# Expert stage of a streaming encoder step: gathers for pairs of experts, 8 KB weight rows, one weight tile of six in plain fp32, unrolled with two accumulator sets

## What is computed

```python
def moe_ffn(h, ...):                       # h: 320 x 1024
    g_p, g_i = top_k(softmax(h @ w_rg + b_rg), 1)          # one of 4 groups
    e_p, e_i = top_k(softmax(logits of that group's 8 experts), 2)
    gate = g_p * e_p / sum(e_p)
    # for each of 32 experts e, for the tokens t routed to it:
    a, u = split(h[t] @ w_e_in[e], 2)      # w_e_in[e]: 1024 x 1024, two halves of 512
    y = ((silu(a) * u) @ w_e_out[e]) * gate                # w_e_out[e]: 512 x 1024
    # y is added back to the token's row; every token has two choices
x = LN2(alpha * x + (1 + gate2) * moe)
```

## Time and profile before

| | |
|---|---|
| runs (us) | 1332.75, 1337.75, 1338.72 |
| span of the profiled execution (us) | 1332.6 |
| time of that execution by itself | not listed beside the runs; its span is 0.15 us under the fastest run |
| PE busy | 1085.3 us, 81% |
| DVE busy | 963.6 us, 72% |
| ACT busy | 694.6 us, 52% |
| POOL busy | 647.2 us, 49% |
| moved by DMA | 303.33 MB, mean 228 GB/s |

### The profile page before, as it was taken

How to read it: one execution, slowest core, us unless ns; L and a number is a source line. 1 busy time by engine, 2 the same in 40 slices (tenths; PEclk the granted TensorE clock), 3 DMA queues, 4 the chain that set the end, 5 groups by cost and what they waited for, 6 DMA issues and landing times.

```text
span 1332.6 us, 14213 instructions
## 1 busy us (share of the span) xinstructions
PE 1085.3 (81%) x4460; PEld 752.7 (56%) x4460; DVE 963.6 (72%) x1069; ACT 694.6 (52%) x734; POOL 647.2 (49%) x348
## 2 busy tenths in 40 slices
PE   5688899888999999998845788888888788888850
PEld 2355677566786666686634555555555565555540
DVE  3968642456653333456785999999999999999967
ACT  3654231231322222332223688888888788888842
POOL 0423920200010000001804999998999979998740
PEclk8798999998997555697956999999999999999885
DMA  9676333244636100136424799999999999999923
GB/s 333 241 256 233 110 111 135 85 137 146 229 92 214 63 0 0 63 127 205 130 103 124 267 370 363 370 364 367 368 366 366 370 353 366 374 366 368 355 97 118
DMA packets 151813, 303.33 MB, mean 228 GB/s; under 512 B 10740, under 2 KB 10788, under 8 KB 151270
## 3 DMA queue, kind: packets, MB, share of 16 engines
q1 hardware_dynamic: 142040, 282.75, 60.1%
q0 software_dynamic: 9744, 20.19, 5.1%
HBM read 299.97 MB, written 14.73 MB: 236 GB/s over the span
## 4 chain that ended last, share of the span: by engine, by line
PE 33%; POOL 24%; DMA 17%; issue 12%; DVE 10%; ACT 2%; POOLq 1%; SPq 0%; ACTq 0%; DVEq 0%
POOL x_item L732 10%; DMA x_item<-scratch_h,slot_token_now 9%; PE bank L1671 6%; PE bank L1677 6%; PE bank L1673 4%; DMA w_raw<-in_w_in 3%; POOL scratch_y L743 2%; POOL slot_token_now L728 2%; POOL slot_row_now L739 2%; DVE w_lo L1033 2%; PE bank L1704 2%; ACT w_hi L782 1%; DMA scratch_y<-y_item,slot_row_now 1%; DMA w_raw<-in_w_ada 1%; PE bank L1829 1%
## 5 line engine op out<-in xcount | busy, mean ns | idle before, releaser
L1538 DVE TENSOR_TENSOR w_lo<-w_raw,w_hi 128x2048 fp32r<-128x2048 f32 x188 | 432.8, 2315 | 15.6 <-ACT w_hi L939 15.6
L939 ACT ACTIVATE w_hi<-w_raw 128x2048 fp32r<-128x2048 f32 x188 | 354.9, 1904 | 2.1 <-PE bank L1943 1.4
L1033 DVE TENSOR_TENSOR w_lo<-w_raw,w_hi 128x2048 fp32r<-128x2048 f32 x72 | 173.3, 2425 | 136.6 <-ACT w_hi L782 136.4
L782 ACT ACTIVATE w_hi<-w_raw 128x2048 fp32r<-128x2048 f32 x72 | 136.6, 1912 | 209.0 <-PE bank L1677 92.4
L1943 PE MATMUL bank<-w_lo,xT_item 128*128 128x512 f32 x512 | 155.5, 426 | 89.9 <-DVE w_lo L1538 89.9
L732 POOL DMA_INDIRECT x_item<-scratch_h,slot_token_now x32 | 218.5, 6829 | 15.9 <-DMA scratch_y<-y_item,slot_row_now 11.4
L1943 PEld LDWEIGHTS bank<-w_lo,xT_item 128*128 128x128 f32 x512 | 89.0, 192 | 154.8 <-DVE w_lo L1538 142.0
L1940 PE MATMUL bank<-w_hi,xT_item 128*128 128x512 f32 x512 | 149.2, 414 | 6.5 <-ACT w_hi L939 2.6
L1671 PE MATMUL bank<-w_hi,h_hi 128*128 128x512 f32 x384 | 142.1, 411 | 12.7 <-ACT w_hi L782 12.3
L1940 PEld LDWEIGHTS bank<-w_hi,xT_item 128*128 128x128 f32 x512 | 93.4, 192 | 39.4 <-issue 17.0
L728 POOL COPY slot_token_now<-slot_token 64x1 int32 (+1 forms) x32 | 107.7, 3366 | 5.7 <-DMA x_item<-scratch_h,slot_token_now 5.6
(11 more groups left out here) (438 smaller groups left out, 1753.4 us busy)
## 6 DMA issues: line engine op xcount, KB each, us to landing
w_raw<-in_w_e_in SPq DMA_DIRECT2D x128, 1024.0 KB, 5.6
w_raw<-in_w_e_out SPq DMA_DIRECT2D x64, 1024.0 KB, 6.3
w_raw<-in_w_in SPq DMA_DIRECT2D x32, 1024.0 KB, 8.0
w_raw<-in_w_ada SPq DMA_DIRECT2D x24, 1024.0 KB, 6.6
bias_rows<-in_b_in SPq DMA_DIRECT2D x16, 256.0 KB, 4.8
w_raw<-in_w_ret_proj SPq DMA_DIRECT2D x4, 1024.0 KB, 19.2
w_raw<-in_w_fox_proj SPq DMA_DIRECT2D x4, 1024.0 KB, 20.7
w_raw<-in_w_o SPq DMA_DIRECT2D x4, 1024.0 KB, 5.1
```

The lines of the kernel that those rows point to most:

```text
L782: nc.scalar.activation(whi[n % NSPL][:], raw[n % NRAW][:], ACT.Copy).then_inc(hi_done, 1)
L939: nc.scalar.activation(whi[ss][:], raw[rs][:], ACT.Copy).then_inc(hi_done, 1)
L1033: V.tensor_tensor(wlo[n % NSPL][:], raw[n % NRAW][:], whi[n % NSPL][:].bitcast(F32), ALU.subtract).then_inc(lo_done, 1)
L1538: V.tensor_tensor(wlo[ss][:], raw[rs][:], whi[ss][:].bitcast(F32), ALU.subtract).then_inc(lo_done, 1)
```

## The change

The expert stage is written anew:

- Items are experts in a fixed order in which two neighbours form a pair (`expert_of`: 0, 16, 1, 17, ...). One gather brings up to 128 rows, 64 for each of the two, into one of two `xg` buffers, and one scatter takes 128 result rows from one of two `ySb` buffers. POOL's copies of index columns and its `hold` instructions are gone for these.
- The weights' rows are dealt to partitions in blocks ("(p k) n" in place of "(k p) n"), so that a tile is one run of 8 KB a partition in place of four of 2 KB. To match, DVE stores h2 (L1393) and the hidden rows (L1552) permuted.
- A tile j of w_e_in now holds all 1024 columns of two rows a partition, so each of the tiles 0 to 3 feeds both banks, a and u. Tile 2 (`NATIVE`) is not split: PE multiplies it as fp32, with the unsplit 64 rows (`xR`) as the stationary operand.
- The loops are unrolled. a and u have two sets of banks (0, 1 and 2, 3, by the item's parity), the result uses banks 4 and 5, `hidden_T` writes bank 5, and the pair's rows are transposed into banks 6 and 7.
- The splitting of expert 0's tiles in the router's stretch is gone. The rows that come back for the closing stage land in the space of the raw tiles.
- An expert's further items, of which there are none in this data, run in a loop behind.

The diff, cut to its core. First the weights' layout and the order of the loads on SP's queue:

```diff
-    w_in_e = i["w_e_in"][0].rearrange("e (k p) n -> e p k n", p=P)
+    w_in_e = i["w_e_in"][0].rearrange("e (p k) n -> e p k n", p=P)
...
+        for e in range(NE + 1):
+            if e < NE:
+                for j in range(4):
+                    expert_tile(e, j)
+            if e:
+                for j in (4, 5):
+                    expert_tile(e - 1, j)
```

POOL's loop over pairs; a gather of pair q waits for the transposes of pair q-2, a store for the four sums of its pair:

```diff
+        for q in range(2, PAIRS):
+            pool.wait_ge(x_landed, 16 * q)
+            gather(q)
+            if q - 2 < 3:
...
+            if q >= 3:
+                pool.wait_ge(y_written, 16 * (q - 3))
+            store_pair(q - 2)
```

ACT (n counts the split tiles alone, m all tiles):

```diff
+            m, n = tile_at[(e, j)], split_at[(e, j)]
+            act.wait_ge(raw_landed[m % NRAW], 16 * (m // NRAW + 1))
+            act.wait_ge(used, n - NSPL + 1)
...
+        def x_high(q):
+
+            act.wait_ge(x_trans, q + 1)
+            nc.scalar.activation(xR[q % 2][:].rearrange("p k c s -> p (k c s)"), bank[7][:, 0:4 * SLOTS],
+                                 ACT.Copy).then_inc(x_raw, 1)
+            nc.scalar.activation(xT[q % 2][:, 4:6, :, 0:SLOTS], pair_of(bank[7], 4)[:, 2:4], ACT.Copy)
+            nc.scalar.activation(xT[q % 2][:, 0:4, :, 0:SLOTS], pair_of(bank[6], 4), ACT.Copy).then_inc(x_hi, 1)
...
+        for e in range(NE + 1):
+            if e < NE:
+                item_hi(e, 0)
+            if e:
+                lows(e - 1)
+            if e < NE:
+                item_hi(e, 1)
+            if e:
+                silu(e - 1)
+            if e < NE:
+                item_hi(e, 3)
+            if e >= 2:
+                y_low(e - 2)
+            if e:
+                hidden_high(e - 1)
+                item_hi(e - 1, 4)
+                item_hi(e - 1, 5)
+            if e % 2 == 0 and e + 2 < NE:
+                x_high(e // 2 + 1)
```

DVE (the permuted store of h2 first):

```diff
-            st(V.tensor_tensor(ht, ht, m2[0:rows, 0, :], ALU.add), h2_ready)
...
+            st(V.tensor_tensor(ht.rearrange("r (k p) -> r p k", p=P), tmp.rearrange("r (p k) -> r p k", p=P),
+                               m2[0:rows, 0, :].rearrange("r (p k) -> r p k", p=P), ALU.add), h2_ready)
...
+        for e in range(NE + 1):
+            if e < NE:
+                item_lo(e, 0)
+            if e:
+                sums(e - 1)
+            if e < NE:
+                item_lo(e, 1)
+            if e:
+                hidden(e - 1)
+            if e < NE:
+                item_lo(e, 3)
+            if e >= 2:
+                y_sum(e - 2)
+            if e:
+                hidden_low(e - 1)
+                item_lo(e - 1, 4)
+                item_lo(e - 1, 5)
+            if e % 2 == 0 and e + 2 < NE:
+                x_low(e // 2 + 1)
```

PE (`in_product(j)` and `out_product(j)` are eight matmuls of 512 columns, four by `hi` and four by `lo`, and then count up `used`):

```diff
+        def native_product(e, b, X):
+
+            m = tile_at[(e, NATIVE)]
+            pe.wait_ge(raw_landed[m % NRAW], 16 * (m // NRAW + 1))
+            for kk in range(2):
+                for half in range(2):
+                    last = mm(bank[b + half][0:SLOTS, :], X[kk], wide(raw[m % NRAW])[:, kk, 512 * half:512 * half + 512],
+                              start=False, stop=False)
+            last.then_inc(nat_used, 1)
...
+            if e < NE:
+                pe.wait_ge(x_split, q + 1)
+                if e >= 2:
+                    pe.wait_ge(u_drained, e - 1)
+                in_product(0)
+                in_product(1)
+            if e:
+                if e >= 2:
+                    pe.wait_ge(y_drained, 2 * (e - 1))
+                hidden_T(e - 1)
+            if e < NE:
+                pe.wait_ge(x_raw, q + 1)
+                native_product(e, ab, [xR[q % 2][:, kk, c, :] for kk in range(2)])
+                in_product(3)
+            if e:
+                pe.wait_ge(hh_split, e)
+                out_product(4)
+            if e % 2 == 0 and e + 2 < NE:
+                x_transpose(q + 1)
+            if e:
+                out_product(5)
```

More of the change, by code:

```diff
@@ L521, in _, with expert_tile @@
[L521 to L524, removed]
-                         w_out_e[bass.ds(last, 1), :, :, 512 * j:512 * j + 512].rearrange("e p k n -> (e p) k n")
-                         ).then_inc(raw_landed[slot_of(j)[0]], 16)
+        def expert_tile(e, j):
+            m = tile_at[(e, j)]
+            sp.wait_ge(*freed[m - NRAW])
+            sp.dma_start(wide(raw[m % NRAW]), tile_source(expert_of(e), j)).then_inc(raw_landed[m % NRAW], 16)
@@ L1927, in _, with x_transpose, split_product @@
         last.then_inc(f, 1)
[L1930 to L1931 removed]
+        def x_transpose(q):
+            pe.wait_ge(x_landed, 16 * (q + 1))
             for k in range(KD):
[L1933 to L1934 removed]
+                last = tr(bank[6 + k // 4][:, P * (k % 4):P * (k % 4) + P], xg[q % 2][:, P * k:P * k + P], ident)
             last.then_inc(x_trans, 1)
[L1937 removed]
+        def split_product(n, b, slot, X, first, final):
@@ L1938, in product @@
             pe.wait_ge(hi_done, n + 1)
-            for kk in range(4):
-                mm(bank[b][:, :], X[:, kof + kk, :], whi[ss][:, kk, :], start=(first and kk == 0), stop=False)
+            for kk in range(2):
+                for half in range(2):
+                    mm(bank[b + half][:, :], X[kk], wide(whi[slot])[:, kk, 512 * half:512 * half + 512],
+                       start=(first and kk == 0), stop=False)
             pe.wait_ge(lo_done, n + 1)
-            for kk in range(4):
-                last = mm(bank[b][:, :], X[:, kof + kk, :], wlo[ss][:, kk, :], start=False, stop=(final and kk == 3))
+            for kk in range(2):
+                for half in range(2):
+                    last = mm(bank[b + half][:, :], X[kk], wide(wlo[slot])[:, kk, 512 * half:512 * half + 512],
+                              start=False, stop=(final and kk == 1))
@@ L1948, in hidden_T @@
             for k in range(4):
-                step = tr if k else mm
-                last = step(bank[5][:, SLOTS * k:SLOTS * k + SLOTS], hid[:, P * k:P * k + P], ident[0:SLOTS, 0:SLOTS])
+                last = tr(bank[5][:, SLOTS * k:SLOTS * k + SLOTS], hid[:, P * k:P * k + P], ident[0:SLOTS, 0:SLOTS])
             last.then_inc(h_tr, 1)
-        def out_product(e, n0_, j0):
-            pe.wait_ge(hh_split, e + 1)
-            for j in range(2):
-                product(n0_ + j, slot_of(j0 + j)[1], 2 + j, hdT, 0, True, True)
+        pe.wait_ge(slt_done, 1)
```

465 lines of the change are left out of this document (251 added, 214 removed).

## The result

The changed kernel takes 1471.38 us (median of 4 runs, 1468.90 to 1474.29) against 1335.25 us for the kernel before on the same chip (4 runs, 1331.45 to 1338.72): a ratio of 1.1025 with a 95% interval of 1.0995 to 1.1054. It is slower by 10%. The forecast was 1491, the range 1400 to 1540. The profiled execution took 1470.25 us, its span is 1468.4.

A forecast was written before the change was run, and what follows sets the result against it. DVE was taken to bound the kernel before, a ring through PE, ACT and DVE the changed one; 14 even items of 25.35 us and 15 odd of 20.5 make 662 us, +154 on the span, 1491 us, range 1400 to 1540.

The forecast's parts named there:

- The ring: Once-per-item chain of waits through DVE, PE and ACT, from y_sum round to y_sum: 17.9 us odd, 22.75 even, at full clock.
- The x transposes: PE's eight transposes for the next pair, behind out_product(4) in even items: 8 x 0.193 = 1.54 us.
- The clock: PE's 3.0 us wait per item halves its clock for part of the work behind it: 2.6 us lost per item.
- the argument that 1.71 us was enough: Earlier PE wait of 1.71 us at a late gather was followed by clock 0.50, so 3.0 us waits should be too.
- The permuted store of hidden: DVE's store of hidden in every item: 0.60 us taken, up to 1.20 if a stride halves DVE's rate.
- The fp32 tile: PE's native product on the unsplit tile, in every item: 3.6 us at full clock, between 3.4 and 4.6.
- The hand-over and x_high in even items: ACT's x_high copies standing before hi(e+1, 0), with the hand-over: 1.31 us.
- The signs: Expected in the changed profile: DVE 65 to 75% busy, PE waiting for y_item, lowered clock, alternating items, DMA under 330 GB/s.
- The parts costed at nothing: 8 KB rows, the gather (issued about 26 us ahead), two bank sets and unrolling: taken to change nothing or next to nothing.
- The ring at full clock: Rival: PE's 3.0 us waits might not lower the clock each time; 1414 us, chance 0.17.
- The two others: Rivals: clock not recovering or gather late, about 1570 us, chance 0.07; transfers as the bound, about 1338 us, chance 0.04.
- The rival of the other side: DVE stays the bound, items of 14.9 us, 1256 us; needs under 5.2 us outside DVE; chance 0.04.

The follow-up runs named there:

- experiment 1: Changed kernel with the hidden transposes moved to bank 6 and PE's wait for the y sums moved ahead of out_product(4): 1315.54 us, ratio 0.9851.
- experiment 2: Changed kernel with the next pair's eight x transposes moved ahead of PE's wait for the y sums: 1402.14 us, ratio 1.0507.
- experiment 4: Changed kernel with three of the fp32 tile's four products left out (six of eight matmuls): 1395.88 us, ratio 1.0453.
- experiment 7: Changed kernel with ten unread matmuls in PE's wait, hidden stored plainly and output weights read in 4 KB rows: 1413.09 us, ratio 1.0577.
- experiment 3: Changed kernel with ten matmuls whose result nobody reads put in PE's wait for the y sums: 1421.75 us, ratio 1.0650.
- experiment 11: Changed kernel with a new order on PE, DVE and ACT, and input weights in 4 KB rows: 1273.42 us, ratio 0.9546.
- experiment 9: Changed kernel with the new order on PE, DVE and ACT, hidden stored plainly and PE's transposes reading every fourth column: 1288.80 us, ratio 0.9662.
- experiment 10: Changed kernel with the new three-engine order, plain hidden store and all expert weights in 4 KB rows: 1287.11 us, ratio 0.9649.
- experiment 8: Changed kernel with only the order of work on PE, DVE and ACT changed; same loads, tiles and arithmetic: 1275.07 us, ratio 0.9549.
- experiment 5: Changed kernel with DVE storing hidden plainly and PE's transposes reading every fourth column: 1470.26 us, ratio 1.1020.

## Why the prediction was right

**The ring** is what the trace shows, step by step and in the order that the prediction gave, and experiments 1, 2, 4 and 7 each change the time through one of its steps. The forecast had 20.5 us for odd and 25.35 for even items; 20.2 and 24.17 were measured. The odd item comes this close in part by luck: 0.5 to 0.6 us too much for the clock and 0.32 too little for the store of hidden nearly cancel. The first `w_lo` of items 2 and 31 and the last y sums on DVE, after:

```profile
748.77 2.29 DVE L1604 TENSOR_TENSOR w_lo<-w_raw,w_hi 128x2048 fp32r<-128x2048 f32 x1 [0.94 <-ACT w_hi L965]
...
1395.13 2.29 DVE L1604 TENSOR_TENSOR w_lo<-w_raw,w_hi 128x2048 fp32r<-128x2048 f32 x1 [2.86 <-ACT w_hi L965]
...
1429.34 1.28 DVE L1640 TENSOR_TENSOR y_pair<-bank,y_low 64x512 f32<-64x512 f32 x2 [2.77 <-ACT y_low L987]
```

Of the 20 us by which 1491 was too long, the 29 items between these two `w_lo` make 15.6 (662 us forecast, 646.4 measured), the earlier start of item 2 (748.8, not 753) 4.2; the end from there (35.5 us against 34.2) goes the other way by 1.3.

**The mis-sized terms.**
- The x transposes: 1.54 us forecast from the earlier trace rows, 0.79 measured. The 24 of the earlier trace rows were run at the start of the kernel, 0.193 us each; here one takes 0.10.
- The clock: 2.6 us an item forecast as half of a mean slow stretch. The tile took 5.35 to 5.5 us against 3.58 at the upper clock, start to start, and the transposes 0.62 against 0.39: 2.0 to 2.1 us. By the four windows above the clock stood low for 4.6 x 0.50 + 3.4 + 4.0 x 0.28 = 6.8 us, as long as in the earlier trace rows, but 2.3 us of it lay in the wait itself; half of the other 4.5 is lost. With the wait filled (experiment 3) the fp32 tile begins at 1097.57, 1119.60 and 1137.82 in turn: items of 22.0 and 18.2 us, the same 2.0 to 2.1 less. That each wait would bring the fall held for the 3.1 to 3.25 us of the changed kernel; the argument that 1.71 us was enough is no rule, since in experiment 2 the same wait of 2.25 us was followed by the slow tile in nine items and by the fast one in five.
- The permuted store of hidden: 0.60 taken, 0.92 from start to start (1.08 in all) measured. The far end of its bounds, 1.20, was nearer in kind; the range held it.
- The fp32 tile: 3.6 us at full clock taken between 3.4 and 4.6; 3.65 in experiments 1 and 3, 3.58 of it from its start to the next. So the extra 0.15 us of the earlier trace rows is not paid at each matmul; that it is the reload of the operand is not shown.
- The hand-over and x_high in even items, 1.31 us: 1.30.

**The signs** all came: DVE 69% busy, its `lo` waiting for ACT, ACT for PE, PE for y_pair once per item, a clock of 0.85, items that alternate (by 4 us, not 5), 285 GB/s.

**The parts costed at nothing.** 8 KB rows: right in the ring, and by experiment 11 also without it. The gather was covered: it landed 3.4 us after its issue, not 13 to 26. POOL's two operations for the closing norm, which the sum left out, stand beside the two odd items of 22.1 us, 1.9 more than the others (under experiments 9 and 10). The two accumulator sets and the unrolling were not tried apart.

**The rivals.** The ring at full clock is experiment 3: 1422 us against 1414. The two others did not come: the clock is back at 1.00 behind the fp32 tile, and the transfers stand at 285 GB/s. The rival of the other side, DVE as the bound with 1256 us, names what a free order gives: experiments 8 and 11 reach 1275 and 1273. It failed in the changed kernel where the prediction said that it would, at the ring's part outside DVE: 10.2 us in odd items (limit 5.2). The change's saving on DVE was real; the order of the queues took it away.

## What to carry to other kernels

When work is taken from the engine that bounds a kernel, follow the semaphores once round for each item before counting the gain: a wait that nobody felt while that engine was full can close a ring through three engines. Look for the buffer whose release starts the ring, and move that one wait, or give it a bank of its own, before anything is made shorter. Where TensorE's clock falls in a wait, as it did here, the wait costs twice, so work that must be done anyway (the next transposes) belongs into it.

## What the runs showed of the hardware that was not expected

- Ten matmuls without use made the kernel 50 us faster (experiment 3), and a shorter wait of PE (2.9 instead of 3.2 us in the mean) was followed by a slower fp32 tile, 890 instead of 850 ns a matmul (experiment 5). The same wait of 2.25 us was followed by either clock (experiment 2).
- POOL's indirect gather holds its queue 1.0 us in the changed kernel, where DVE is often idle, and 2.8 us in experiment 8, where DVE is at 97%.
- A `tensor_tensor` of DVE that scatters its 64 x 512 fp32 results takes 1079 ns, with a plain store 676.
- DVE and POOL look as if they held each other up, either way round: POOL 8.27 us and DVE 2.2 us a `lo` in experiment 8, POOL 2.41 us and DVE up to 4.80 in experiment 9. No run tried this by itself.
- 404 to 414 GB/s over hundreds of us from one core, within 1% the same with the input weights in rows of 4 or 8 KB (experiments 8 and 11). A DMA share near 1.00 does not say that the transfers are the bound: it read 0.97 at 383 GB/s and 1.01 at 414.
